# Second banks and buffers in the output stage's first tiles, earlier first loads, and a later score row in a hybrid attention and mixture-of-experts block

## What is computed

```python
mixed = mix_groups(...)             # 4 differential heads (2 softmaxes each) and 8 grouped heads, over 1280 keys
x = x + gt1 * rmsnorm(mixed @ w_out, g_post_mix)
h2 = modulate(rmsnorm(x, g_pre_ffn), sh2, sc2)
s = sigmoid(h2 @ w_router)          # then group-limited top 8 of 64 experts
y = sum over chosen experts e of w_e * swiglu(h2, w_eg[e], w_eu[e], w_ed[e]) + swiglu(h2, w_sg, w_su, w_sd)
x = x + gt2 * rmsnorm(y, g_post_ffn)
```

## Time and profile before

| | |
|---|---|
| median of 3 runs | 2186.69 us (2185.58 to 2186.93) |
| the profiled execution | 2190.17 us |
| its span in the trace | 2188.4 us |
| mean granted TensorE clock | 0.965 |
| PE, DVE, ACT, POOL busy | 91%, 72%, 62%, 43% |

### The profile page before, as it was taken

One profiled execution on the slowest core, in us unless ns is written; L12 is line 12 of the kernel. 1 busy time (PEld: TensorE's weight loads), 2 busy tenths in 40 slices (PEclk: granted clock), 3 DMA queues, 4 the chain that ended last, 5 costly groups with the idle time before them and its releaser, 6 DMA issues.

```text
span 2188.4 us, 36315 instructions
## 1 busy us (share of the span) xinstructions
PE 2000.5 (91%) x9592; PEld 1492.9 (68%) x9592; DVE 1575.2 (72%) x2206; ACT 1353.4 (62%) x1952; POOL 941.0 (43%) x869
## 2 busy tenths in 40 slices
PE   4899997889989899789989999999999999999993
PEld 2676666555656555567638888888877888888881
DVE  3852374675557655456438999999988999999995
ACT  2422122555556555322328998898877998889982
POOL 1010111651135310025444666566655666666663
PEclk8999998899999999889999999999999999999997
DMA  7464346812131111458439999799999978789967
GB/s 264 140 180 138 116 135 165 242 39 44 37 63 37 30 42 27 173 122 160 108 108 313 316 363 303 227 279 314 351 334 344 350 226 221 223 240 367 290 152 259
DMA packets 162651, 429.16 MB, mean 196 GB/s; under 512 B 26993, under 2 KB 82033, under 8 KB 137889
## 3 DMA queue, kind: packets, MB, share of 16 engines
q1 hardware_dynamic: 92818, 294.36, 37.4%
q0 software_dynamic: 60048, 116.89, 24.1%
q10 hardware_dynamic: 9712, 16.99, 2.8%
HBM read 360.83 MB, written 96.26 MB: 209 GB/s over the span
## 4 chain that ended last, share of the span: by engine, by line
PE 43%; DMA 7%; DVE 3%; issue 3%; ACT 2%; SPq 1%; ACTq 1%; POOL 0%; DVEq 0%; POOLq 0%
PE ps_d L2072 10%; PE ps_r L2055 7%; PE ps_r L2057 7%; PE ps_r L2056 7%; DMA w_experts<-in_w_exp_down 5%; PE ps_y L1978 4%; PE ps_y L2045 3%; PE ps_g L1995 2%; PE ps_d L2012 1%; DMA y_scratch<-e_y,e_target_index 1%; PE ps_g L2079 1%; ACT w_gate_up_high L1592 1%; ACTq L1305 1%; DVE w_gate_up_low L1823 0%; PE ps_t L1958 0%
## 5 line engine op out<-in xcount | busy, mean ns | idle before, releaser
L1823 DVE TENSOR_TENSOR w_gate_up_low<-w_experts,w_gate_up_high 128x1024 fp32r<-128x1024 f32 x416 | 489.3, 1217 | 18.7 <-ACT w_gate_up_high L1592 18.6
L1592 ACT ACTIVATE w_gate_up_high<-w_experts 128x1024 fp32r x416 | 416.6, 1049 | 31.4 <-SPq L1350 12.9
L2055 PE MATMUL ps_r<-w_gate_up_high,gatheredT_high 128*128 128x512 f32 x832 | 336.9, 405 | 2.7 <-DVE gatheredT_low L1829 2.7
L2057 PE MATMUL ps_r<-w_gate_up_high,gatheredT_low 128*128 128x512 f32 x832 | 327.5, 394 | 0.0
L2056 PE MATMUL ps_r<-w_gate_up_low,gatheredT_high 128*128 128x512 f32 x832 | 325.6, 391 | 0.0
L1481 POOL DMA_INDIRECT y_scratch<-e_y,e_target_index x104 | 277.3, 2667 | 108.5 <-POOL e_target_index L1477 93.0
L969 DVE TENSOR_REDUCE neg_max<-ps_scores 128x1 f32<-128x1280 f32 x128 | 190.2, 1490 | 172.6 <-PE ps_scores L1064 172.2
L1858 DVE TENSOR_TENSOR w_down_low<-w_experts,w_down_high 128x2048 fp32r<-128x2048 f32 x103 | 236.1, 2293 | 48.8 <-ACT w_down_high L1617 48.0
L1467 POOL DMA_INDIRECT gathered<-h_scratch,e_gather_index x106 | 198.7, 1874 | 95.3 <-POOL e_gather_index L1464 90.2
L1617 ACT ACTIVATE w_down_high<-w_experts 128x2048 fp32r x103 | 197.9, 1921 | 36.8 <-issue 36.8
L2055 PEld LDWEIGHTS ps_r<-w_gate_up_high,gatheredT_high 128*128 128x128 f32 x832 | 157.5, 189 | 35.5 <-issue 6.1
(11 more groups left out here) (282 smaller groups left out, 3840.2 us busy)
## 6 DMA issues: line engine op xcount, KB each, us to landing
w_experts<-in_w_exp_gate SPq DMA_DIRECT2D x64, 1024.0 KB, 9.2
w_experts<-in_w_exp_up SPq DMA_DIRECT2D x64, 1024.0 KB, 12.6
w_experts<-in_w_exp_down SPq DMA_DIRECT2D x64, 1024.0 KB, 17.0
w_mod_later<-in_w_mod ACTq DMA_DIRECT2D x32, 512.0 KB, 3.7
w_mod_first<-in_w_mod SPq DMA_DIRECT2D x4, 2048.0 KB, 15.6
w_in_raw<-in_w_in SPq DMA_DIRECT2D x32, 256.0 KB, 3.7
values<-in_tokens SPq DMA_DIRECT2D x10, 512.0 KB, 11.3
k_high_low<-k_scratch POOLq DMA_DIRECT2D x8, 640.0 KB, 7.0
```

Source lines behind the costliest of these rows:

```text
L1592: act.activation(split_slice(eH, j), raw_slice(ring, slot, j), ACT.Copy).then_inc(X["wH"], 1)
L1823: nc.vector.tensor_tensor(split_slice(eL, j), raw_slice(ring, slot, j), split_slice(eH, j).bitcast(F32), ALU.subtract).then_inc(X["wL"], 1)
L2055: nc.tensor.matmul(psR[:], xH[:, k], eH[:, k], start=(k == 0), stop=False)
L2057: last = nc.tensor.matmul(psR[:], xL[:, k], eH[:, k], start=False, stop=(k == KD - 1))
```

## The change

It does seven things.

1. The second score row of a grouped unit u+1 is made right after `tr(u, 0)`, not at the end of unit u-1. ACT's and DVE's lists stay as they are.
2. Within attention, at unit 18, SP loads the last quarter of w_out, tile 0 of `o_scratch` and the first x tile (into bytes that differential keys had), and the wait for all stores of `o_scratch` moves from attention's end into the output stage, ahead of the load of tile 4.
3. Projections 1 and 3 go to the banks of ps_d, the others stay in ps_y. `proj(t)` waits for `residual` number 1, 2, 3 (counted from one) for t = 2, 3, 4, and for number t from t = 5 on; `shared_down(0)` waits for number 4.
4. oT_high and oT_low get a second buffer. DVE's `low_o(t+1)` waits for the projection of tile t-1 only.
5. PE's round becomes `proj(t, 0)` with `logits(t-2)` in its middle, `turn_o(t+1)`, `proj(t, 1)`, `turn_h(t-1)`, then as before; in round 8 `logits(6)`, `turn_h(7)`, `logits(7)`. `turns` and ACT's list follow: `squares(t, 0)`, `out_o(t+1)`, `squares(t, 1)`, `out_h(t-1)`.
6. SP's loads: of the shared weights one follows the load of tile 2, two the load of tile 3; the early expert loads go ahead of a round's stores, at rounds 2, 3, 4, 5, 6 and 8.
7. At the start ACT and DVE handle the first transposed tile after one chunk of w_out, not after two.

```diff
@@ attention, SP
+                if u == last_diff + 3:
+                    sp.wait_ge(s_s, row0[last_diff + 1])
+                    sp.dma_start(w_rest[:], a["w_out"][0, wa.shape[1] * P:, :]...).then_inc(s_rest, 16)
+                    for w in s_od:
+                        sp.wait_ge(w, (DH + GKV) // 2 * 16)
+                    sp.dma_start(o_first[:], o_d[0:P, :]).then_inc(s_of_tile, 16)
+                    sp.dma_start(x_first[:], a["tokens"][CTX:CTX + P, :]).then_inc(s_xr, 16)
-            sp.wait_ge(s_od[0], ((NU + 1) // 2) * 16)
-            sp.wait_ge(s_od[1], (NU // 2) * 16)
@@ attention, PE
                     tr(u, kt)
+                    if kt == 0 and u + 1 < NU and second_row_late(u + 1):
+                        qk(u + 1, 1)
...
-                        if kt == KT_N - 1:
+                        if kt == KT_N - 1 and not second_row_late(u + 2):
                             qk(u + 2, 1)
@@ tail
-        oH = b.at("oT_high", [P, KD, P], F32R, 136 * K)
-        oL = b.at("oT_low", [P, KD, P], F32R, 140 * K)
+        oH = [b.at(f"oT_high{u}", [P, KD, P], F32R, at) for u, at in enumerate((136 * K, 120 * K))]
+        oL = [b.at(f"oT_low{u}", [P, KD, P], F32R, at) for u, at in enumerate((140 * K, 124 * K))]
...
+            if t + 1 < NT:
+                turns += [("o", t + 1, 0), ("o", t + 1, 1)]
             if 1 <= t <= NT:
                 turns += [("h", t - 1, 0), ("h", t - 1, 1)]
-            if t + 1 < NT:
-                turns += [("o", t + 1, 0), ("o", t + 1, 1)]
...
-        AHEAD_OF = {1: (0, (0,)), 2: (0, (1,)), 3: (0, (2,)), 4: (1, (0,)), 5: (1, (1,)), 6: (1, (2,))}
+        AHEAD_OF = {2: (0, (0,)), 3: (0, (1,)), 4: (0, (2,)), 5: (1, (0,)), 6: (1, (1,)), 8: (1, (2,))}
+        def ps_proj(t):
+            return psD if t in (1, 3) else psY
+        def freed_by(t):
+            return 0 if t < 2 else t - 1 if t <= 4 else t
@@ tail, DVE
-                    dve.wait_ge(S["proj"], 2 * t + 2)
+                    if t >= 1:
+                        dve.wait_ge(S["proj"], 2 * t)
                     low_o(t + 1)
@@ tail, PE
-                if t >= 1:
-                    pe.wait_ge(S["x1"], t)
+                if freed_by(t):
+                    pe.wait_ge(S["x1"], freed_by(t))
                 for k in range(KD):
+                    if h == 0 and k == KD // 2 and 2 <= t:
+                        logits(t - 2)
...
                 if t < NT:
                     proj(t, 0)
-                if 1 <= t <= NT:
-                    turn_h(t - 1)
+                if t + 1 < NT:
+                    turn_o(t + 1)
                 if t < NT:
                     proj(t, 1)
-                if t + 1 < NT:
-                    turn_o(t + 1)
+                if t == NT:
+                    logits(NT - 2)
                 if 1 <= t <= NT:
-                    logits(t - 1)
+                    turn_h(t - 1)
+                if t == NT:
+                    logits(NT - 1)
```

## The result

| | before | after |
|---|---|---|
| median, same chip | 2186.43 us (7 runs, 2180.63 to 2186.93) | 2172.88 us (7 runs, 2169.06 to 2182.54) |
| ratio | | 0.9939, 95% interval 0.9924 to 0.9954 |
| profiled execution, its span | 2190.17, 2188.4 us | 2173.62, 2171.7 us |

The changed kernel is 13.6 us faster. Two more comparisons on two other chips gave 0.9930 [0.9908, 0.9951] and 0.9955 [0.9938, 0.9973]: 15.6 and 12.2 us between the medians, 15.4 and 9.9 us by the ratios. The prediction was 28.7 us: right in sign, twice too large, and outside its range (2150 to 2170).

A forecast was written before the change was run, and what follows sets the result against it. PE bounds most of the kernel, with slack in the output stage up to tile 5's projection. 7.8 + 5.0 + 18.7 - 2.8 = 28.7 us gained, median 2158 us; own range 2152 to 2165, with rivals 2150 to 2170.

The forecast's parts named there:

- Start, banks, first four rounds: Output stage: first projection 5.0 us earlier; projection 0 to 4 gains 21.9 us; PE idles 2.3 us in round 2.
- Part 1: Attention: the moved second score row fills PE's wait for an exp, 0.77 us in most grouped units; 7.8 us gained in sum.
- The fourth differential unit: Attention, each half: transposes wait for DVE's mix, then the moved row and its exp come later; 1.5 us lost, twice.
- Loads: Output stage: loads have more time than they need to land; cost nothing unless shared weights hold up SP's queue.
- Rounds 5 to 7: Output stage, tiles 5 to 7: stay bound by PE at the old 25.8 us each; nothing gained.
- Round 4: Output stage: PE idles from E + 47.8 to 51.4, and low clock adds 1.4 us; tile 5 starts at E + 61.5.
- The end: Output stage, round 8: logits(6) behind the shared gate delay the route of tile 6 by logits and exp; 2.8 us lost.
- A: Output stage: clock stays low in a part of every round through new waits of 1 to 4 us; 2169.5 us, chance 0.12.
- B: Attention: the moved row gives nothing, since ACT's in-order list returns what PE wins; 2166 us, chance 0.12.
- D: Output stage: rounds don't overlap and stay at 20.7 us; gain only 10 us, time 2177 us, chance 0.05.
- E: Attention: moved row exposed in full in all 16 units, 3.4 us each; slower, 2220 us, chance 0.05.
- C: Output stage: POOL's scattered DMAs are quicker, three rounds each up to 2.4 us shorter; 2151 us, chance 0.10.

The follow-up runs named there:

- one_bank: Changed kernel with every projected tile in the one pair of banks (ps_y) again; buffers, order and loads kept. Ratio 0.9975 to the kernel before.
- again2: The changed kernel once more, without an edit, on another chip. Ratio 0.9955 to the kernel before.
- no_scatter: Changed kernel with slot numbers of tiles 0 to 3 not stored, only the output stage read. Projection 4 to 5 in 25.9 us, 5 to 7 in 53.2.
- again: The changed kernel once more, without an edit, on another chip. Ratio 0.9930 to the kernel before.
- logits_back: Changed kernel with logits of tile 6 taken in round 7 again. Ratio 0.9887 to the kernel before; projection 7 to first expert down 103.6 us.
- row_only: Kernel before with only the second score row of grouped units made later. Ratio 0.9972 to the kernel before, 6.1 us faster.

## Why the prediction was half the truth

Of 28.7 us, 15.1 did not come: 6.0 at the end of the stage, 6.3 in rounds 4 to 6, 2.9 in attention.

**Start, banks, first four rounds: right.** Projection 0 comes 4.9 us sooner (said 5.0), and 0 to 4 takes 59.3 to 63.1 us (said 61.0). PE waits for the low half ahead of the turn in rounds 2 (2.05 us, said 2.3) and 4; in round 3, where the text named it too, it doesn't. one_bank shows that the second banks remove the waits on the residual.

**Part 1, mis-sized: 4.9 instead of 7.8.** Grouped units lie 16.10 us apart (said 16.15), ten times, which gives 8.3 us. The four units with other terms gave nothing. From copy to copy, the first grouped unit of each half takes 16.66 instead of 16.50 us (said 0.5 gained), the seventh of the first half 19.88 instead of 19.62 (said 1.3 gained), the seventh of the second 14.31 instead of 13.42 (said 0.77 gained), and so in all 18 profiles with the later row: 1.4 lost where 3.1 were added. The rows show why. In the two sevenths the kernel before had no wait for an exp, so there was no hole to close, and in all four a new wait for DVE's copy stands near the start, 0.87 and 0.46 us in these two (first grouped unit of the first half, seventh of the second):

```profile
514.78 0.66 PE L1084 MATMUL ps_scores<-ident,probs 128*128 128x128 f32 x4 [0.87 <-DVE probsT L997]
```

```profile
863.85 0.66 PE L1084 MATMUL ps_scores<-ident,probs 128*128 128x128 f32 x4 [0.46 <-DVE probsT L997]
```

The fourth differential unit was to lose 1.5 us a half. From copy to copy it lost 1.1 to 3.9, but the unit ahead of it, which no longer makes the row, gained 1.6, so the pair lost 1.2 on average (from 0.4 gained to 2.3 lost). What varies there is the clock. Busy time of that unit, before, after and again2, one fence each:

```profile
484.00:507.80 23.80, 19.52 (x90) 11.88 (x89) 9.69 (x12) 11.70 (x20) 3.53 (x5) 1.00 0.16 34
```

```profile
486.00:511.30 25.30, 20.44 (x90) 13.16 (x91) 10.21 (x12) 11.78 (x20) 3.53 (x5) 0.93 0.15 32
```

```profile
482.00:509.60 27.60, 22.04 (x90) 14.06 (x90) 10.14 (x12) 11.77 (x21) 3.53 (x5) 0.88 0.14 29
```

The same 90 matmuls take 20.4 to 22.0 instead of 19.5 us, as the clock falls to 0.93 and 0.88. I had priced the new wait there and not the clock behind it, though I priced it so in round 4; with the gain of the unit ahead left out too, the 3.0 came near the measured 2.4 by luck. The first differential unit of the second half moved as well, from 0.9 us lost to 1.2 gained, which no term had.

**Loads, the step that failed in round 4.** "The x tiles have more than their 5.2" took the median of the earlier trace rows, from rounds of 20.7 us, and put the loads at nothing. A median says nothing of the load that matters: before's own slowest x_in took 17.6 us, in round 4, where the DMA engines stood at 0.93. In the changed kernel it took 22.0 and 23.5. Rounds 3 to 5 ask for the same transfers, and the same scattered stores, in less time. In no_scatter, where nothing is late, round 4 takes 25.9 us, even less than the 26.6 forecast, against 30.7 on average: so the late transfers account for the 4.0 us missed there. Of the 2.3 in rounds 5 and 6 they account for 0.8 (53.2 against 54.0). I named this risk for tile 2 and the shared weights, gave it no price and no chance; it was tile 4, and the scattered stores of place.

**Rounds 5 to 7, put at nothing, cost some 0.7 us each.** With every transfer in time (no_scatter) such a round still takes 26.6 us, not the old 25.8, and round 6 does so in all profiles of the new order that keep DVE's list. The turn of h2 now stands right ahead of the turn of the shared act, and PE waits for ACT's copy of it (round 6 of the kernel after; before has no such wait):

```profile
1024.11 0.41 PE L2028 MATMUL ps_t<-ident,gate_a 128*128 128x128 f32 x2 [0.48 <-ACT h2T L1560]
```

**Round 4 beside that.** The wait (said 3.6) was 2.9 us in two of the three profiles. Its clock was priced at half a slow half, 1.4 us; in the first profile the gate took 2.1 us more than in before and the transposes 0.9 more, in again2 0.8 and 0.9, in again nothing. Low clock and late x_in partly cover each other, so neither has a price of its own.

**The end, mis-sized, the largest miss: 8.8 instead of 2.8.** The place was right (logits(6) behind the gate), the sum took only the logits and the exp. Left out were the table load behind them (1.28), silu's table and two copies ahead of logits(7), the lower clock after 3.44 us of idle PE, POOL's memset beside the route, and round 7's own 1.0. logits_back gives back 7 us. Some 1 us of the 8.8 belongs to no edit: the step of 43.3 instead of 41.7 us in two of the three profiles.

**The rivals.** A gave 2169.5, the nearest time, but for a reason that did not come: after the first projection the clock is 1.00 in rounds 1 to 3 and 5 to 7 of the profile shown. The low clock came in three places instead, round 4, the end, and attention. By the rule quoted from the Trainium skill (TensorE: Matmul & The Clock Gate; A second HAM failure mode: psum-queue depth-cycling) it should have swung in every round; here it didn't, and where the same page (HAM oscillation) tells of one kernel without gain from double-buffered PSUM, one_bank shows some 10 us here. B fell with row_only, D with the starts of the projections, E with both. C's condition did not come: the first scattered DMA of tiles 0 and 1 still took 2.62 and 2.70 us. The forecast and A to D add up to 0.95, not to the 0.94 of the text. The 3.5 us taken off for the profiled execution were right for before, 3.7 above its median; after's lay 0.7 above, so the gain between the two profiled executions (16.6 us) is 3 us larger than that between the medians.

## What to carry to other kernels

When rounds get shorter, look again at every transfer in them: take the slowest landing, from the stretch with the highest DMA share, not the median, and ask what small scattered transfers run beside it. When an instruction moves past a wait, follow all that queues behind it on the next engine, table loads among it, look at what the moved work will now run beside, and price the low clock after every new idle spell of PE of some 3 us. Before pricing a hole once per unit, check that every unit has it. If three things end within a few us of each other, mending one only shows the next.

## What was not expected of the hardware

- Scattered 4-byte stores that use 3.0% of the DMA engines beside SP's transfers raise the landing of a 512 KB load from 4.3 us (median, at most 7.7) to as much as 23.5 us in round 4; in round 6, with as many stores, it is 4.1 (again2).
- A DVE step on 128x64 takes 2.51 to 2.54 us instead of 0.20 beside a memset on POOL, in all eleven profiles where the two meet.
- ACT's square in round 4 began some 7 us late in three of 20 profiles, all with the later expert loads, its wait ended by an event that the trace calls remote. Open.
- The front stage, the same in all kernels, ends within a spread of 7 us.
